# Linear attention's pair products: 128-row products with zero-filled queries in place of 64-row ones

## The reference

```
def gla_chunked(q, k, v, gk):
    """S_t = diag(exp(gk_t)) S_{t-1} + k_t v_t^T,  o_t = S_t^T q_t."""
    ...
    Bc = jnp.cumsum(gc, axis=-2)
    ...
    dec = jnp.where(causal, jnp.exp(jnp.where(causal, diff, 0.0)), 0.0)
    attn = jnp.einsum("bhnid,bhnjd,bhnijd->bhnij", qc, kc, dec)
```

## Time and profile before

| | |
|---|---|
| median of 3 runs | 2085.93 us |
| lowest, highest | 2083.0, 2086.07 us |
| profiled execution | 2079.45 us |
| its span, first to last instruction | 2077.7 us |
| mean granted TensorE clock in it | 0.985 |
| instructions | 27850 |
| TensorE busy | 1980.7 us, 11438 instructions |

### The profile page before, as it was taken

How to read it: one execution, slowest core, us unless ns; L and a number is a source line. 1 busy time by engine, 2 the same in 40 slices (tenths; PEclk the granted TensorE clock), 3 DMA queues, 4 the chain that set the end, 5 groups by cost and what they waited for, 6 DMA issues and landing times. The chain is left out here.

```text
span 2077.7 us, 27850 instructions
## 1 busy us (share of the span) xinstructions
PE 1980.7 (95%) x11438; PEld 1573.5 (76%) x11438; DVE 1158.4 (56%) x1454; ACT 850.1 (41%) x1212; POOL 309.7 (15%) x258
## 2 busy tenths in 40 slices
PE   8999899899988989898999999999999999999998
PEld 5677896577777768655778888886788878888886
DVE  4446556654656553276478547735563557745753
ACT  4236433523643351265354324424345444423432
POOL 0200523120051320044220000022000012000002
PEclk9999999999999999999999999999999999999999
DMA  6111103221110222210232232233221203232321
GB/s 237 64 67 53 42 2 122 101 80 63 41 43 34 89 93 90 95 37 1 81 101 95 85 107 89 83 110 125 98 82 61 76 28 110 80 104 102 102 84 69
DMA packets 30786, 167.70 MB, mean 81 GB/s; under 512 B 2827, under 2 KB 9635, under 8 KB 14916
## 3 DMA queue, kind: packets, MB, share of 16 engines
q1 hardware_dynamic: 30228, 165.13, 22.7%
q10 hardware_dynamic: 432, 0.79, 0.1%
HBM read 159.58 MB, written 10.00 MB: 82 GB/s over the span
## 5 line engine op out<-in xcount | busy, mean ns | idle before, releaser
L313 PE MATMUL psum<-inputs_high,weights_high 128*128 128x512 f32 x928 | 384.9, 415 | 17.3 <-DVE inputs_low L261 9.4
L315 PE MATMUL psum<-inputs_high,weights_low 128*128 128x512 f32 x928 | 366.7, 395 | 0.0
L314 PE MATMUL psum<-inputs_low,weights_high 128*128 128x512 f32 x928 | 366.6, 395 | 0.0
L2180 PE MATMUL psum<-inputs_high,weights_high 128*128 128x512 f32 x704 | 276.2, 392 | 0.5 <-DVE inputs_low L2324 0.5
L2181 PE MATMUL psum<-inputs_low,weights_high 128*128 128x512 f32 x704 | 274.0, 389 | 0.0
L2182 PE MATMUL psum<-inputs_high,weights_low 128*128 128x512 f32 x704 | 274.0, 389 | 0.0
L266 DVE TENSOR_TENSOR weights_low<-weights_raw,weights_high 128x2048 fp32r<-128x2048 f32 x66 | 154.7, 2343 | 162.0 <-ACT weights_high L255 162.0
L313 PEld LDWEIGHTS psum<-inputs_high,weights_high 128*128 128x128 f32 x928 | 175.6, 189 | 76.8 <-DVE inputs_low L261 13.8
L314 PEld LDWEIGHTS psum<-inputs_low,weights_high 128*128 128x128 f32 x928 | 176.0, 190 | 41.2 <-issue 5.7
L315 PEld LDWEIGHTS psum<-inputs_high,weights_low 128*128 128x128 f32 x928 | 175.7, 189 | 40.5
L255 ACT CAST weights_high<-weights_raw 128x2048 fp32r<-128x2048 f32 x66 | 125.3, 1899 | 153.6 <-PE psum L315 137.8
(11 more groups left out here) (403 smaller groups left out, 3168.8 us busy)
## 6 DMA issues: line engine op xcount, KB each, us to landing
weights_raw<-w_stream SPq DMA_DIRECT2D x116, 1024.0 KB, 4.8
weights_raw<-w_down SPq DMA_DIRECT2D x32, 704.0 KB, 4.1
residual_parked<-residual SPq DMA_DIRECT2D x2, 2048.0 KB, 10.7
residual_back<-residual_parked SPq DMA_DIRECT2D x2, 2048.0 KB, 7.7
residual<-x_t SPq DMA_DIRECT2D x2, 1024.0 KB, 9.9
bias_by_row<-bias_rows SPq DMA_DIRECT2D x2, 1024.0 KB
bias_by_row<-bias_rows SPq DMA_DIRECT2D x1, 1536.0 KB
out_t<-residual SPq DMA_DIRECT2D x5, 256.0 KB, 2.0
```

Source lines behind the costliest of these rows:

```text
L313: pe.matmul(out, hi, self.ahi[:, k], start=start and b == 0, stop=False)
L314: pe.matmul(out, hi, self.alo[:, k], start=False, stop=False)
L315: mm = pe.matmul(out, lo, self.ahi[:, k], start=False, stop=stop and b == blocks - 1)
L2180: pe.matmul(out, wh, hi, start=start, stop=False)
```

## The change

The queries of a level are written by GpSimd in another layout. In `apart_q`, the 64 queries of a tile stand packed, once for each of the two heads of the tile: 64 columns for the head of the lower partitions, then 64 columns for the other. In a head's columns, the partitions of the other head hold zeros, which GpSimd writes once at the phase's start. A pair product of a level is then two products (one for each pair of heads) that contract 128 rows, with 128 columns, in place of four that contract 64 rows with 64 columns. The diagonal's pair products stay as they were.

GpSimd multiplies the queries in two operations, one for each half of the partitions. All scores of a level's pair product now fit in one PSUM bank, and four banks are used in turn, so from j = 5 on `pair(j)` waits for an earlier copy.

```diff
+        apart_q = qs.rearrange("p s f (t y i) -> p s (f t) y i", t=TT, y=2)
...
         def pair_bank(j):
-            return 4 + 2 * (j % 2)
+            return 4 + (2 * (j % 2) if j < TT else j % 4)
+
+        def taken_by(j):
+
+            return j - 1 if j <= TT else max(j - 3, 3 if j == TT + 1 else 0, 4 if j == TT + 2 else 0)
...
                     if n:
-                        pe.wait_ge(s.scaled, 2 * n)
+                        pe.wait_ge(s.scaled, 3 * n)
+                        if j < 2 * TT:
+                            pe.wait_ge(s.zeroed, 2)
                     else:
                         pe.wait_ge(s.freed, TT)
                     if j >= 2:
-                        pe.wait_ge(s.taken, j - 1)
+                        pe.wait_ge(s.taken, taken_by(j))
...
-                    for hd in range(HEADS):
-                        rows = slice(64 * (hd % 2), 64 * (hd % 2) + 64)
-                        if n:
-                            ka, qa, wide = ks[:, (n - 1) % 2], qs[:, (n - 1) % 2], P // 2
-                            moving = qa[rows, hd // 2, cols].rearrange("p (b i) -> p b i", i=2 * LEVELS[n - 1])
-                            moving = moving[:, :, LEVELS[n - 1]:]
-                        else:
-                            ka, moving, wide = kk, q[rows, hd // 2, cols], P
-                        f = hd // 2
-                        mm = pe.matmul(ps[:, pair_bank(j) + hd % 2, f * wide:(f + 1) * wide], ka[rows, f, cols], moving,
-                                       start=True, stop=True)
+                    if n:
+                        out = ps[:, pair_bank(j), 0:2 * P].rearrange("p (y f i) -> p f y i", y=2, f=2)
+                        for f in range(2):
+                            mm = pe.matmul(out[:, f], ks[:, (n - 1) % 2, f, cols], apart_q[:, (n - 1) % 2, f * TT + t],
+                                           start=True, stop=True)
+                    else:
+                        for hd in range(HEADS):
+                            rows, f = slice(64 * (hd % 2), 64 * (hd % 2) + 64), hd // 2
+                            mm = pe.matmul(ps[:, pair_bank(j) + hd % 2, f * P:(f + 1) * P], kk[rows, f, cols],
+                                           q[rows, f, cols], start=True, stop=True)
...
-                        src = ps[:, b:b + 2, 0:P].rearrange("p y (c i) -> p y c i", i=size)
+                        src = ps[:, b, 0:2 * P].rearrange("p (y c i) -> p y c i", y=2, i=size)
...
+                def later_queries(v, n):
+                    size = LEVELS[n]
+                    return v.rearrange("p f (t b i) -> p (f t) b i", t=TT, i=2 * size)[:, :, :, size:]
+
+                def queries(n, y):
+                    rows, slot = slice(64 * y, 64 * y + 64), n % 2
+                    here = apart_q[rows, slot, :, y].rearrange("p g (b i) -> p g b i", i=LEVELS[n])
+                    pool.tensor_tensor(here, later_queries(q, n)[rows], later_queries(fall[:, slot], n)[rows],
+                                       ALU.mult).then_inc(s.scaled, 1)
+
...
-                    pool.tensor_tensor(upper(qs[:, slot], n), upper(q, n), upper(fall[:, slot], n), ALU.mult) \
-                        .then_inc(s.scaled, 1)
+                    if n:
+                        pool.wait_ge(s.scaled, 3 * n)
+                    queries(n, 0)
                     pool.tensor_tensor(lower(ks[:, slot], n), lower(kk, n), lower(fall[:, slot], n), ALU.mult) \
                         .then_inc(s.scaled, 1)
+                    pool.wait_ge(s.scaled, 3 * n + 2)
+                    queries(n, 1)
+                for y in range(2):
+                    rows = slice(64 * y, 64 * y + 64)
+                    if y:
+                        pool.wait_ge(s.zeroed, 1)
+                    pool.memset(apart_q[rows, :, :, 1 - y], 0.0).then_inc(s.zeroed, 1)
+                pool.wait_ge(s.zeroed, 2)
```

More of the change, by code:

```diff
@@ L392, in hybrid_projections @@
             nc, *GEMM, "parked", "tap", "conv", "silu", "small", "small_out", "logits", "small_turned", "act_step", "log_f",
-            "sums", "filled", "slot_filled", "apart", "falls", "scaled", "pair", "taken", "end_arg", "end_exp", "k_end",
+            "sums", "filled", "slot_filled", "apart", "falls", "scaled", "zeroed", "pair", "taken", "end_arg", "end_exp", "k_end",
             "turned", "turned_read", "square", "square_sum", "inv_ln", "inv_norm", "normed", "z_silu", "gate_act", "gate_dve",
@@ L730, in _ @@
                     if c == 7:
-                        act.wait_ge(s.scaled, 2 * n_levels)
+                        act.wait_ge(s.scaled, 3 * n_levels)
                         act.wait_ge(s.pair, n_pairs)
@@ L790, in apart @@
                     if n >= 2:
-                        dve.wait_ge(s.scaled, 2 * n - 2)
+                        dve.wait_ge(s.scaled, 3 * n - 3)
                     dve.tensor_tensor(fl, middle, low, ALU.subtract).then_inc(s.apart, 1)
@@ L865, in _ @@
                         elif j == 25:
-                            dve.wait_ge(s.scaled, 2 * (n_levels - 1))
+                            dve.wait_ge(s.scaled, 3 * (n_levels - 1))
                             dve.tensor_tensor(cq[1], cq[0][:, :, P - 1:P].to_broadcast([P, 8, P]), cq[0],
```

## The result

The changed kernel took 2055.32 us (median of 4 runs, 2052.1 to 2065.02) against 2086.0 for the kernel before (4 runs): a ratio of 0.9856, 95% interval 0.9835 to 0.9876. The forecast was 2062 in a range of 2054 to 2073. Two later measurements of the same kernel gave 0.9857 [0.9838, 0.9876] and 0.9863 [0.9843, 0.9883]. Its profiled execution took 2057.55 us, span 2055.8; for that one the sum had said 2055.8.

What follows compares the result with a forecast made beforehand. TensorE, busy for 95% of the span, was taken as the bound. Shorter pair products (19.4 us) and removed waits (4.3) gave 23.7 us, so 2062 us from the median of 2085.93, range 2054 to 2073.

Steps and rivals of the forecast that it cites:

- What bounds the kernel: First layer, 131 to 218 us: TensorE busy 86.93 of 87 us, so time spared before it moves everything forward.
- The cost of a pair product: TensorE's weight stream: a pair falls from 0.79 to 0.43 to 0.45 us, 56 times, 19.4 us saved.
- The waits that go: TensorE's waits for VectorE's copies (line 782): four of six go, 4.28 of 6.8 us, all counted as saved.
- GpSimd's price: Query multiplication per level: three operations for two, 1.29 us each, 3.55 as the upper end.
- 4.9 us at product 24: Tightest cover between GpSimd's query operations and the product needing them: 4.9 us left with one operation more.
- Rival E: GpSimd cannot feed the level products, each 2.0 us late beyond 4.9 of cover; about 2092 us, chance 0.05.
- The zero fills: Two GpSimd fills at a phase's start: 0.9 or 2.6 us each, up to 5.1 us if blocking VectorE; taken as nothing.
- level 0: GpSimd's third operation might precede the subtraction setting the j = 2 wait: 1.3 to 1.5 us per layer; taken as nothing.
- The sum: Whole kernel: 19.4 + 4.3 = 23.7 us saved; 2055.8 from the profiled execution, 2062 from the median.
- rival A: The forecast itself: mode change and waits both go, 2062 us, own range 2056 to 2068, chance 0.72.

Runs made afterwards that it cites:

- e3: Kernel before with each level product contracting all 128 rows, without zeros, still four matmuls of 64 columns in the old banks; ratio to before 1.0014.
- e4: Kernel before with each pair product made in two visits, the second one weight step later; ratio to before 1.0051, 16.9 us more at one clock.
- e5: Kernel before with two pair products back to back in one visit; ratio to before 0.9924, 13.3 us less at one clock.
- the ordinary execution of before: Kernel before, unchanged, profiled once more for an execution at a usual clock; 2087.47 us at a clock of 0.980.
- e1: Changed kernel with the pair products' banks in turn of two again and the old copy wait; ratio to before 0.9921, 6.7 us above the changed kernel at one clock.

## Why the prediction was right

- What bounds the kernel: right. 131 to 218 us was full of TensorE, and what was saved before it stayed saved: no new wait in front of it.
- The cost of a pair product: right in size and cause. 0.43 to 0.45 forecast from lines 501 and 1003, 0.43 to 0.45 measured. The 0.34 us is the row mode's change, by e3, e4 and e5.
- The waits that go: the four went and none took their place. 4.3 us was right for what the kernel before lost by them: the second layer's stretch shrank by 11.4 us, 9.3 for 27 products and 2.1 for its two waits. It is not what four banks are worth in the changed kernel; there two banks would cost 6.7 us of waiting. And a wait can cost clock on top (3.0 us in the ordinary execution of before), for which the sum had no term.
- GpSimd's price: 1.28 us for 64 partitions with 512 elements, as for 128 partitions; right. Where VectorE blocked it, an operation took a few tenths to 2.2 us longer. The cover of "4.9 us at product 24" was the weakest step: it was 3.2 at product 16, and at 24 it was 3.6 (operations done at 97.53, product at 101.16), with the three operations there at 2.43, 1.74 and 1.62 us in place of 1.28. It was enough for one operation more than before and not for three. Rival E's threshold stood 1.7 us too high by that.
- The zero fills, open up to 5.1 us: they took 1.95 us for both and cost nothing. TensorE's wait at the second layer's start was 5.98 again. The third operation did not get ahead of the subtraction at level 0.
- The sum: 23.7 us, and 23.4 at one clock; the pair products' stretches of two profiled executions that both had the short stretch at the lower clock, 11.6 and 11.4 us shorter, give 23.0 without the slope. What it lacked is the clock: nothing in it said that the changed kernel would be granted 0.985 and not 0.9815. Taken from the median of before, 2062 was therefore 6.7 us too high. 2055.32 lies below rival A's own range of 2056 to 2068 and only 1.3 us inside the stated one, whose lower end had no reason of this kind: that the clock's part stayed inside it was luck.
- What stays open: how much of those 6 to 7 us belongs to the change. A part may, for the waits at product 10 are gone. Four profiled executions had them, two each, at 1.4 to 1.9 us (the two of before, e1 and e3), and behind three of the eight the clock fell. e1, which puts them back, falls to 0.981. But only some 1.6 us of its profiled execution are lost to the clock inside the stretches; from 560 to 660 us its clock was 0.90, where the changed kernel had 0.93 to 0.95 and the kernel before 0.98 and 0.91. And e5 has 0.9815 with waits of 1.0 us at most, e4 0.986 with waits of 0.9 at most. I can't settle it from these runs.

## What to carry to other kernels

Small products inside a stream of full-height ones can cost more than their rounds if they use another row mode, as they did here: look for the distance from the product ahead to the second behind, not for durations. A zero-filled full-height product was then cheaper than two half-height ones side by side, with doubled columns that cost nothing more (0.11 us an instruction with 64 columns in e3 and with 128 in the earlier trace rows). Putting several half-height products in one visit was cheaper too. Before giving a helper engine more work, look for its tightest deadline in every level, and count how often another engine's work blocks it. Where executions of one kernel differ with the clock, compare the changed stretch start to start in the traces as well as the medians.

## What the runs showed of the hardware

- Two 64-row fp32 instructions with 64 columns, side by side, keep one pace with one 128-row instruction, 0.11 us a round; the 128-row one takes that with 64 and with 128 columns. Going from 128-row fp32r products to 64-row fp32 ones and back costs 0.34 us a visit, with 4, 8 or 16 instructions in it (0.56, 0.79 and 1.24 us in all).
- GpSimd takes 1.28 us for 512 elements in each of 64 partitions and the same in 128; a zero fill of 64 x 1024 takes about 1.0.
- A wait of 1.52 us was followed by the lower clock in one execution and not in another of the same kernel; of eight waits of 1.4 to 1.9 us at product 10, in four executions, three were. The time of the kernel before goes with its mean clock (0.978 to 0.988 over 44 executions, correlation -0.93), over a spread of 16 us.
- An addition of 16 elements on VectorE took 1.24 us in place of 0.17 behind an operation of GpSimd, and GpSimd's 1.28 became 3.20 behind a subtraction of VectorE.
